# Gate and up projections as seven block products per pair (Strassen's scheme), with the weight sums made by adding transfers within SBUF

## The reference, cut to what matters

```python
def _ffn(x, g, w_gate, w_up, w_down):
    h = _rmsnorm(x, g)
    return x + (jax.nn.silu(h @ w_gate) * (h @ w_up)) @ w_down
```

## Time and profile before

| what | value |
|---|---|
| time, median of 3 runs (lowest, highest) | 955.16 us (954.46, 955.79) |
| the profiled execution's own time / its span | 956.53 us / 954.8 us |
| granted TensorE clock, mean | 0.994 |
| PE busy / DVE / ACT / POOL | 97% / 43% / 37% / 34% of the span |
| moved by DMA | 77.03 MB, mean 81 GB/s |

### The profile page before, as it was taken

The page is one execution under the profiler, slowest core; times in us unless marked ns, Lnnn a source line. Parts: engine busy times, 40 slices in busy tenths (PEclk is TensorE's granted clock), DMA queues, the critical chain, the costliest instruction groups (busy, mean ns, idle before and its releaser), DMA issues.

```text
span 954.8 us, 17920 instructions
## 1 busy us (share of the span) xinstructions
PE 922.7 (97%) x7315; PEld 885.6 (93%) x7315; DVE 410.9 (43%) x850; ACT 351.0 (37%) x641; POOL 327.2 (34%) x139
## 2 busy tenths in 40 slices
PE   3999999999989999999999999999999999999997
PEld 3889999989889888898999999999999999999997
DVE  5582656557783446565443343331123331123311
ACT  5542443535444544544444442222122222122231
POOL 2442313222232223232333344444444444444450
PEclk9999999999998999999999999999999999999999
DMA  8323222121422121212152222323222233232222
GB/s 238 89 71 85 57 77 68 56 78 45 109 67 61 51 68 46 67 47 66 45 178 71 85 80 86 87 85 106 84 73 88 88 88 90 87 89 77 66 57 71
DMA packets 140786, 77.03 MB, mean 81 GB/s; under 512 B 2832, under 2 KB 139494, under 8 KB 140726
## 3 DMA queue, kind: packets, MB, share of 16 engines
q1 hardware_dynamic: 134262, 71.88, 26.4%
q10 hardware_dynamic: 6464, 4.29, 1.7%
HBM read 71.87 MB, written 3.60 MB: 79 GB/s over the span
## 4 chain that ended last, share of the span: by engine, by line
PE 81%; DVE 11%; ACT 4%; issue 2%; DMA 1%; ACTq 1%; SPq 0%; DVEq 0%
PE G L488 24%; PE G L490 23%; PE G L489 22%; PE X L657 2%; DVE qAT L1331 2%; PE X L641 2%; PE X L628 1%; ACT prob L979 1%; DVE rs L1131 1%; DVE rs L1132 1%; DVE rt L1133 1%; ACT rs L904 1%; DVE prob L1356 1%; PE X L584 1%; ACT rt L905 1%
## 5 line engine op out<-in xcount | busy, mean ns | idle before, releaser
L466 POOL TENSOR_TENSOR w_lo<-wraw,w_hi 128x1024 fp32r<-128x1024 f32 x129 | 325.5, 2523 | 603.6 <-ACT w_hi L817 603.4
L488 PE MATMUL G<-h_hi,w_hi 128*128 128x272 f32 x1280 | 385.3, 301 | 4.7 <-DVE rv L1294 2.3
L490 PE MATMUL G<-h_hi,w_lo 128*128 128x272 f32 x1280 | 372.1, 291 | 0.0
L489 PE MATMUL G<-h_lo,w_hi 128*128 128x272 f32 x1280 | 370.3, 289 | 0.0
L488 PEld LDWEIGHTS G<-h_hi,w_hi 128*128 128x128 f32 x1280 | 243.1, 190 | 15.4 <-issue 12.3
L489 PEld LDWEIGHTS G<-h_lo,w_hi 128*128 128x128 f32 x1280 | 243.6, 190 | 0.6
L490 PEld LDWEIGHTS G<-h_hi,w_lo 128*128 128x128 f32 x1280 | 242.8, 190 | 0.0
L488 PE MATMUL G<-f_hi,w_hi 128*128 128x272 f32 x704 | 203.0, 288 | 0.0
L490 PE MATMUL G<-f_hi,w_lo 128*128 128x272 f32 x704 | 202.9, 288 | 0.0
L489 PE MATMUL G<-f_lo,w_hi 128*128 128x272 f32 x704 | 202.1, 287 | 0.0
L817 ACT ACTIVATE w_hi<-wraw 128x1024 fp32r<-128x1024 f32 x129 | 135.3, 1049 | 89.2 <-PE G L490 89.1
(11 more groups left out here) (223 smaller groups left out, 917.8 us busy)
## 6 DMA issues: line engine op xcount, KB each, us to landing
wraw<-in_w_in_dram SPq DMA_DIRECT2D x53, 512.0 KB
wraw<-in_w_gate_dram SPq DMA_DIRECT2D x22, 512.0 KB
wraw<-in_w_up_dram SPq DMA_DIRECT2D x22, 512.0 KB
wraw<-in_w_down_dram SPq DMA_DIRECT2D x16, 512.0 KB
xtok<-in_x_prompt_dram SPq DMA_DIRECT2D x8, 512.0 KB, 5.0
wraw<-in_w_out_dram SPq DMA_DIRECT2D x8, 512.0 KB
wraw<-in_w_down_dram SPq DMA_DIRECT2D x8, 384.0 KB
out_dram<-ytok ACTq DMA_DIRECT2D x8, 256.0 KB, 2.3
```

The lines of the kernel that those rows point to most:

```text
L466: pool.tensor_tensor(w_lo[:, slot, :, :], wraw[:, slot, :, :], w_hi[:, slot, :, :].bitcast(F32), ALU.subtract).then_inc(w_split, 1)
L488: pe.matmul(o, w_hi[:, slot, kc, :], b_hi[:, kc, cols], start=(kc == 0), stop=False)
L489: pe.matmul(o, w_hi[:, slot, kc, :], b_lo[:, kc, cols], start=False, stop=False)
L490: mm = pe.matmul(o, w_lo[:, slot, kc, :], b_hi[:, kc, cols], start=False, stop=(kc == last))
```

## The change: what it does

Of a pair, gate and up are seen as the two block rows of one product, the 1024 inputs as two halves k1 and k2 (4 chunks each, `HK`), and the 544 rows as two halves of 272. Strassen's scheme (in the form with seven products and shared sums) computes the 2 x 2 blocks with seven block products of 4 chunks each in place of eight. So a pair is 7 x 4 x 3 = 84 matmuls of 272 columns in place of 96.

- Four sums of weight blocks are needed per pair. ACT writes a copy and two negated copies (`negatives`, `last_negative`), and POOL issues four DMAs with accumulate, 128 x 512 float32 (256 KB) each, from SBUF to SBUF: two together (`first_sums`), one behind both (`second_sum`), one behind that and behind `last_negative` (`last_sum`). The up tile's k1 half is changed in place in `wraw`. `csum` is double buffered, `csum4` is single.
- The high parts of the sums are ACT's. All low parts of a pair (gate tile, up tile, two sums, and the last sum apart) go from POOL to DVE. POOL keeps the low parts of the other tiles.
- The sums over the activations are made once, in the output stage: `ffn_input` writes 2 blocks per chunk for chunks 0 to 3 and 5 blocks for chunks 4 to 7, which ACT rounds and DVE splits.
- Banks: a pair uses four half buffers; even pairs take the two `G`, odd pairs the two `X`. The order of the products is P1, P5, P6, P7, P2, P4, P3. P2 adds onto P1's bank behind ACT's copy of P1 (`copy_p1`), P4 onto P7's bank once DVE has read it, and P3 onto P5's bank likewise. DVE reads each product and adds it up (`evict_...`, seven instructions of 272 columns).
- A weight slot of a gate tile is freed for its next load by the tile's low part and by `last_negative` of the same pair (`raw_free`). The loop over pairs is written out in place of a hardware loop.
- The residual is loaded by columns, in eight small steps, in place of whole rows at once, and its first load waits for `gb_used`, the last gate of the mixer. Two early merged chunks in place of three (`EARLY`). DVE adds a down tile in two instructions in place of one (times half of `rt`, then the add).

The diff, cut to its core:

```diff
+PAIRS = [(g, GU0[g] + 2 * i) for g, m in enumerate(FF_GROUPS) for i in range(m)]
+FIRST = [sum(FF_GROUPS[:g]) for g in range(len(FF_GROUPS))]
+PAIR_OF = {}
+for _q, (_g, _n) in enumerate(PAIRS):
+    PAIR_OF[_n] = PAIR_OF[_n + 1] = _q
+    USES[_n] = USES[_n + 1] = 0
...
-EARLY = 3
+EARLY = 2
...
+        def raw_free(eng, n):
+            before = n - RING
+            if before in PAIR_OF:
+                q = PAIR_OF[before]
+                eng.wait_ge(pair_lo, 3 * q + (1 if PAIRS[q][1] == before else 2))
+                if PAIRS[q][1] == before:
+                    eng.wait_ge(neg4_ok, q + 1)
+            else:
+                eng.wait_ge(w_split, gemms(before + 1))
...
+            def first_sums(q):
+                r1 = (PAIRS[q][1] + 1) % RING
+                pool.wait_ge(neg_ok, 2 * q + 2)
+                pool.dma_start(csum[q % 2][:, 0], wraw[:, r1, HK:KC, :], accum_op=ALU.add).then_inc(s1_ok[q % 2], 16)
+                pool.dma_start(wraw[:, r1, 0:HK, :], csum[q % 2][:, 1], accum_op=ALU.add).then_inc(s3_ok[q % 2], 16)
+            def second_sum(q):
+                pool.wait_ge(s1_ok[q % 2], 16 * (q // 2 + 1))
+                pool.wait_ge(s3_ok[q % 2], 16 * (q // 2 + 1))
+                pool.dma_start(csum[q % 2][:, 1], csum[q % 2][:, 0], accum_op=ALU.add).then_inc(s2_ok[q % 2], 16)
+            def last_sum(q):
+                pool.wait_ge(neg4_ok, q + 1)
+                pool.wait_ge(s2_ok[q % 2], 16 * (q // 2 + 1))
+                pool.dma_start(csum4[:, :, :], csum[q % 2][:, 1], accum_op=ALU.add).then_inc(s4_ok, 16)
...
+            lows(range(GU0[0]))
+            for g, m in enumerate(FF_GROUPS):
+                q0 = FIRST[g]
+                first_sums(q0)
+                second_sum(q0)
+                first_sums(q0 + 1)
+                last_sum(q0)
+                second_sum(q0 + 1)
+                for q in range(q0, q0 + m):
+                    if q + 2 < q0 + m:
+                        first_sums(q + 2)
+                    if q + 1 < q0 + m:
+                        last_sum(q + 1)
+                    if q + 2 < q0 + m:
+                        second_sum(q + 2)
+                lows(range(DN0[g], DN0[g] + KC))
...
+            def product(bank, a_hi, a_lo, b_hi, b_lo, adds=False, ready=None):
+                for kc in range(HK):
+                    if ready is not None:
+                        pe.wait_ge(f_ok, ready + kc + 1)
+                    pe.matmul(bank, a_hi[:, kc, :], b_hi[:, kc, :], start=(kc == 0 and not adds), stop=False,
+                              skip_group_check=adds)
+                    pe.matmul(bank, a_hi[:, kc, :], b_lo[:, kc, :], start=False, stop=False, skip_group_check=adds)
+                    mm = pe.matmul(bank, a_lo[:, kc, :], b_hi[:, kc, :], start=False,
+                                   stop=(kc == HK - 1), skip_group_check=adds)
+                mm.then_inc(prod_done, 1)
...
+                if q >= 2:
+                    pe.wait_ge(evicted, 6 * (q - 1))
+                if q == 1:
+                    pe.wait_ge(norm_done, len(NORMS) + 1)
+                if q == FIRST[g] and g == 0:
+                    pe.wait_ge(set_free[1], uses_before(n))
+                elif q == FIRST[g]:
+                    for r in range(2):
+                        pe.wait_ge(set_free[(n + r) % 2], uses_before(n + r))
+                pe.wait_ge(pair_lo, 3 * q + 1)
+                product(b1, w_hi[:, r0, k1], w_lo[:, r0, k1], fa_hi[:, :, 0], fa_lo[:, :, 0],
+                        ready=now(0))
+                pe.wait_ge(pair_lo, 3 * q + 3)
+                product(b5, c_hi[s][:, 0], c_lo[s][:, 0], fa_hi[:, :, 1], fa_lo[:, :, 1])
+                if q == 0:
+                    pe.wait_ge(set_free[0], uses_before(n + 1))
+                product(b6, c_hi[s][:, 1], c_lo[s][:, 1], fb_hi[:, :, 3], fb_lo[:, :, 3], ready=now(HK))
+                if q == 0:
+                    x2_squares()
+                product(b7, w_hi[:, r1, k1], w_lo[:, r1, k1], fb_hi[:, :, 2], fb_lo[:, :, 2])
+                pe.wait_ge(p1_ok, q + 1)
+                product(b1, w_hi[:, r0, k2], w_lo[:, r0, k2], fb_hi[:, :, 0], fb_lo[:, :, 0], adds=True)
+                pe.wait_ge(evicted, 6 * q + 2)
+                product(b7, w_hi[:, r1, k2], w_lo[:, r1, k2], fb_hi[:, :, 4], fb_lo[:, :, 4], adds=True)
+                pe.wait_ge(evicted, 6 * q + 3)
+                pe.wait_ge(c4_lo_ok, q + 1)
+                product(b5, c4_hi, c4_lo, fb_hi[:, :, 1], fb_lo[:, :, 1], adds=True)
...
+            def negatives(q):
+                _, n = PAIRS[q]
+                for r in (n, n + 1):
+                    act.wait_ge(wload[r % RING], 32 * (r // RING + 1))
+                if q >= 2:
+                    act.wait_ge(pair_lo, 3 * (q - 1))
+                    act.wait_ge(s4_ok, 16 * (q - 1))
+                act.activation(csum[q % 2][:, 0], wraw[:, (n + 1) % RING, 0:HK, :], ACT.Copy).then_inc(neg_ok, 1)
+                act.activation(csum[q % 2][:, 1], wraw[:, n % RING, 0:HK, :], ACT.Copy, scale=-1.0)\
+                    .then_inc(neg_ok, 1)
+            def last_negative(q):
+                _, n = PAIRS[q]
+                if q >= 1:
+                    act.wait_ge(c4_lo_ok, q)
+                act.activation(csum4[:, :, :], wraw[:, n % RING, HK:KC, :], ACT.Copy, scale=-1.0)\
+                    .then_inc(neg4_ok, 1)
...
+                    more = q + 1 < FIRST[g] + m
+                    if q > FIRST[g]:
+                        gate_tanh(q - 1)
+                    copy_p1(q)
+                    high_part(PAIRS[q + 1][1] if more else DN0[g])
+                    if q > FIRST[g]:
+                        mid_high_part(q - 1)
+                    if q + 2 < FIRST[g] + m:
+                        negatives(q + 2)
+                    last_sum_high_part(q)
+                    if more:
+                        up_high_part(q + 1)
+                        sums_high_part(q + 1)
+                        last_negative(q + 1)
+                    else:
+                        high_part(DN0[g] + 1)
...
+                if i == KC - 4:
+                    negatives(0)
+                    last_negative(0)
+                if i == KC - 2:
+                    high_part(GU0[0])
+                    up_high_part(0)
+                    sums_high_part(0)
+                    negatives(1)
...
+                was = x2T[:, c - HK, :]
+                dve.tensor_scalar(fin[:, 0, :], x2T[:, c, 0:TH], gain(c), None, ALU.mult)
+                link(dve.tensor_scalar(fin[:, 1, :], x2T[:, c, TH:T], gain(c), -1.0, ALU.mult, ALU.mult))
+                link(dve.scalar_tensor_tensor(out=fin[:, 2, :], in0=was[:, TH:T], scalar=gain(c - HK),
+                                              in1=fin[:, 1, :], op0=ALU.mult, op1=ALU.add))
+                link(dve.scalar_tensor_tensor(out=fin[:, 3, :], in0=was[:, 0:TH], scalar=gain(c - HK),
+                                              in1=fin[:, 2, :], op0=ALU.mult, op1=ALU.subtract))
+                dve.tensor_tensor(fin[:, 4, :], fin[:, 0, :], fin[:, 3, :], ALU.subtract).then_inc(fin_ok, 1)
...
-                        dve.wait_ge(gemm_done, i * RING + (n + 1))
-                        dve.tensor_tensor(h2(fg[:, r, :]), halves(G[s]), h2(rt[:, :]), ALU.mult)\
-                            .then_inc(set_free[s], 1)
...
+                for q in range(FIRST[g], FIRST[g] + m):
+                    more = q + 1 < FIRST[g] + m
+                    if q > FIRST[g]:
+                        gated(q - 1)
+                    if more:
+                        low_parts(q + 1, 0)
+                    evict_6(q)
+                    if q > FIRST[g]:
+                        mid_low_part(q - 1)
+                    evict_7(q)
+                    last_sum_low_part(q)
+                    evict_2(q)
+                    if more:
+                        low_parts(q + 1, 1)
+                    evict_4(q)
+                    if more:
+                        low_parts(q + 1, 2)
+                    evict_3(q)
```

More of the change, by code:

```diff
@@ L103, with gemms @@
 USES += [1] * (N_TILES - N_IN)
+PAIRS = [(g, GU0[g] + 2 * i) for g, m in enumerate(FF_GROUPS) for i in range(m)]
[4 more added lines that the diff above has]
+    USES[_n] = USES[_n + 1] = 0
+HK = KC // 2
 POST_TILES = [n for n in range(N_IN) if USES[n] == 2]
+def gemms(n):
+    return sum(m not in PAIR_OF for m in range(n))
 def uses_before(n):
@@ new lines, in _ @@
+            sp.wait_ge(gb_used, KC)
+            sp.wait_ge(qk_done, NU)
+            residual(0)
+            residual(1)
+            for i in range(RING, KC):
+                weights(OUT0 + i, w_out, 0, KC, i * P)
+                residual(i - 2)
+            for g, m in enumerate(FF_GROUPS):
+                for i in range(m):
+                    c = (FIRST[g] + i) * P
+                    weights(GU0[g] + 2 * i, w_gate, 0, KC, c)
+                    weights(GU0[g] + 2 * i + 1, w_up, 0, KC, c)
+                    if g == 0 and i < 2:
```

(3 more changed lines are left out.)

430 lines of the change are left out of this document (254 added, 176 removed).

## The result

The changed kernel took 958.85 us (median of 14 runs, 955.54 to 962.11), the kernel before 954.57 beside it (14 runs). The ratio is 1.0039 with a 95% interval of 1.0025 to 1.0053: slower by 0.4%, where 947.9 and faster was forecast. The profiled execution has a span of 960.4 us, against 954.8 before. It is the longest of the 14 (962.11), so its spans differ by 5.6 us where the medians differ by 4.3.

The account below looks back on a forecast made before the run. PE, busy 97% of the span, bounds the kernel. -33.1 (matmuls) + 7.8 (ring) + 9.9 (start) + 2.5 (clock) + 5.6 (edges) = -7.3 us, from 955.2 to 947.9 us; own range 943 to 953, 8 in 10 937 to 975.

Parts of the forecast that it names:

- What it removes: Feed-forward stage: 12 of 96 matmuls go in each of 22 pairs, at 0.1255 us each: -33.1 us.
- Rival 4: Matmuls get slower, twelve in a row into one bank; 3% gives back 7 us: 955 us, chance 0.03.
- L: Time from `last_negative` to both loads and the transfer being there: 6.2 to 7.8 us, 6.9 taken.
- ring excess: Five of eight pairs at +0.66 us, mean about 10.9, +0.37 for 21 pairs: +7.8 us.
- The ring: From `last_negative` over loads and ScalarE's next instructions to the next `last_negative`: 4.3 us plus L, 11.2 us per pair.
- rival 1: The ring stays under PE's time, so the 7.8 us falls away: 940 us, chance 0.30.
- The adding transfers' latency: POOL's accumulating DMAs: 5 us to land (bounds 2.3 and 10), 1 us to issue; no cost up to 5.9.
- rival 2: Adding transfers are slow: over 7.5 us makes the ring 11.8 us, 8.5 us gives 977 us; chance 0.22.
- VectorE per pair: DVE's fourteen instructions and tanh wait per pair: 9.5 of 10.54 us, nearly full but not the bound.
- The start: Start of the feed-forward part: PE waits for low parts, chunk 7 and the norm's followers: +9.9 us.
- the clock: Reduced PE clock behind two waits of 3 to 4 us at the start, between 0.8 and 6: +2.5 us.
- Edges: Group starts and ends, POOL's low parts meeting DVE, `EARLY` and the last down tile: +5.6 us together.

Follow-up runs that it names:

- experiment 1: Changed kernel with `csum4` in two buffers and `last_negative` moved up in ScalarE's list, nothing left out: 939.21 us, ratio 0.9833 to the kernel before.
- Experiment 4: Changed kernel with one swap in ScalarE's list, `last_negative` ahead of the sums' high part: 960.87 us, ratio 1.0062 to the kernel before.
- experiments 5 and 6: Changed kernel with only the first two adding transfers of a pair halved, then only the later two: 948.85 us and 948.24 us.
- experiments 11 and 14: Kernel with two `csum4` buffers and early `last_negative`, pair 0's copy, high part and evictions moved to cover the norm: 941.46 us; with all adding transfers also halved: 936.91 us.

## Why the prediction was wrong

**What it removes: right.** The matmul's pace didn't change. PE is busy 10.7 us in ring-bound pairs and 10.49 where nothing waits (experiment 1), against 10.54. Rival 4 is out.

**The step that failed is the size of L, with the ring excess that came from it** (+7.8, "L = 6.2 to 7.8. I take the middle, 6.9: the ring is then 11.2 us"). The ring was named rightly, its 4.3 us on ScalarE measured 4.1, and pairs in the middle of a group did run slower, nine of the 21 at over 12 us. But L measured 8.0 to 9.1 and the ring 12.1 to 13.2. For 21 pairs the excess over 10.54 is 242.95 - 221.3 = 21.6 us, 13.8 more than the 7.8. That alone turns the forecast -7.3 into +6.5; the measured difference of the spans is +5.6. (Up to 1.3 of the 13.8 is clock, an estimate of ten matmuls at 0.1255: the 3.4 us at 0.53 in the pair of 13.4 us, shown at the end.) Experiment 1 is the counter-test. It takes the excess away and leaves the other terms, for which the sum says 947.9 - 7.8 = 940.1, rival 1's case; it measured 939.2.

Why L was too small has two parts. The price of an adding transfer is 1.62 us of all 16 engines, 3.2 for two where 3.1 was the upper bound taken, and a load's is 1.85 for 1.6. And the step counted only the two transfers "in the same stretch". Experiment 4 shows that the first two count as well, experiments 5 and 6 that they count alike. The better sum is the DMA work per pair (10.2 us) plus the time in which the ring keeps the DMA engines idle (2.1). It needs prices that no row of before had, and it overrated what halved transfers give, so the idle part is not understood to the end.

**The adding transfers' latency.** Landing took 3.3, 5.1 and 6.2 us at the median, where 5 was taken and "nothing up to 5.9". POOL's issue took 0.84 to 1.19. DVE did not delay that issue, so rival 2's 1.2 us per issue did not come. (Not all of DVE's instructions there have two SBUF inputs, as the rival said: the evictions, `u<-X,p` for one, read a PSUM bank. It changes nothing in the sum.) Nor did its 8.5 us: issue and landing are some 7 at the median. Yet the ring grew past the 11.8 that rival 2 had from 7.5 us on: its direction, by another mechanism, work of the DMA engines in place of one transfer's latency. The estimate of 2.6 us by the formula in the page "DMA: Bandwidth & Descriptors" of the Trainium skill is below every median of the whole transfers.

**VectorE per pair: right.** 8.8 us of busy time (9.5 less 0.8 forecast) and the 0.7 for the tanh.

**The start (+9.9) and the clock (+2.5): right in sum, and almost in place.** Against 559.1 they forecast +10.9 and it was +11.8. Executions differ here: in experiment 4's, whose edit touches nothing that pair 0 waits for, pair 0 began 2.3 us and ended 2.8 us earlier (568.11). The waits of 1.8, 0.7, 3.3 and 4.0 became 2.27, 0.47, 3.07 and 1.63 + 1.45. No reordering won it back by itself; that the DMA work of the next pairs takes the gain is what the pairs of experiments 11 and 14 speak for, and the times don't show it clear of noise.

**Edges (+5.6): 3.9.** PE's waits for DVE at the group starts are 2.0 in all, 1.7 forecast.
